# Gates of a linear recurrence: scaling inside the activations, a convolution tap on another engine, and work moved into the first head

## The chip, the cores and the metric

The kernel runs on one core of a Trainium2 chip. The metric is device time in microseconds, here from three runs of the unchanged kernel: median 2751.18 us, 2739.63 to 2753.92 us. The engines are TensorE (PE in the profile), VectorE (DVE), ScalarE (ACT), GpSimd (POOL) and the queue SyncE (SP).

## What is computed

One inference step of a decoder of two layers, for 512 prompt positions and 8 samples of one position each, 520 tokens in all. A layer projects the normed input with one large matrix, runs a retention branch (4 heads) and a gated linear recurrence (RG-LRU) on parts of the result, merges both, and ends with a SwiGLU block. The change is in the RG-LRU branch, of width 1280:

```
def causal_conv(x, buf, w, b):                   # CONV_W = 4
    xx = jnp.concatenate([buf, x], axis=1)
    y = b
    for j in range(CONV_W):
        y = y + xx[:, j:j + L] * w[j]
    return y, xx[:, -(CONV_W - 1):]

def rg_lru(xc, w_a, b_a, w_x, b_x, lam, h0):     # w_a, w_x block-diagonal, 16 blocks of 80
    r = sigmoid(xc @ w_a + b_a)
    i = sigmoid(xc @ w_x + b_x)
    log_a = -8.0 * r * softplus(-lam)
    a = jnp.exp(log_a)
    u = jnp.sqrt(-jnp.expm1(2.0 * log_a)) * (i * xc)
    # h_t = a_t * h_(t-1) + u_t, from h0
    return h, h[:, -1]
# lru_branch = (gelu(y_lru) * h) @ w_lru_out
```

## The kernel before

Everything lies transposed: 128 channels on the partitions, the 520 tokens along the free axis. Each float32 product is made of three TensorE passes (high x high, high x low, low x high; `product`, L321), so every operand is first split into a rounded high part and the rest. For weights GpSimd does the split, one unit of up to 1024 columns at a time: L307 makes `w_high`, L309 `w_low`, into two buffers that TensorE frees. SyncE loads the raw units. For activations ScalarE writes the high part (a Copy) and VectorE subtracts to get the low part.

Each engine runs an order that is written out by hand, and semaphores tie the engines together. TensorE's order in a layer is: four retention heads (the first in `one_head(0, True)`), two early tiles of the LRU's x branch, the eight output tiles of the last head (`ret_out`, added by VectorE in `ret_add`, L716), then the LRU stage, then merge, output projection and SwiGLU.

The LRU stage has 10 channel tiles, in two groups g of five (t = 0 to 4). For group 0 TensorE runs, for each t: `y` (8 blocks of 128x128, the gelu branch), two gate tiles (2 or 3 blocks each, from the convolved x), and one x tile (8 blocks) of a tile further on (`FILL_X`). Then come the x tiles (1,3) and (1,4), and group 1, where the place of the x tile is taken by output tiles `o` (5 blocks each, `FILL_O`). A block takes six matmuls of 260 columns. Results go through a ring of four PSUM places: the reader of place n must have freed it before TensorE may begin tile n+4. `read_x` (L877), `read_y` (L962) and `read_out` (L1009) on VectorE and the two sigmoids on ScalarE (L1300, L1303) are the readers.

For a tile c = 5g + t the work off TensorE is:

- `read_x`, then `conv`: the last tap with the bias (L894), three small copies for the outputs (L896 to L898), then per remaining tap one scalar_tensor_tensor over the prompt (L902) and one over the 8 sample columns (L904). ScalarE makes the high part (`conv_high`, L1291), VectorE the low part (`conv_low`, L911).
- ScalarE: two sigmoids. VectorE: `use_gates` multiplies r by the channel's 8 softplus (L969) and i by x (L972). ScalarE: a = exp(-.) (L1308), tanh (L1310), gelu of y (L1312). VectorE: `one_less_a2`, a squared (L979), then (a squared + 1) times tanh, which is 1 - a squared (L981). ScalarE: sqrt (L1314).
- VectorE: `scan` (L987 to L997) with a copy of the last columns (L995), then the split of the gated result (L1295, L1002).

Four of ScalarE's functions in this chain need a table load: sigmoid, exp (tanh shares it), gelu, sqrt. In VectorE's order `scan(g, t-1)` stands in the iteration of t. The softplus is a series (L919, L921, terms 19 down to 1 on 128x10), made by VectorE between the eight `ret_add`, from an exponential that ScalarE makes after the last head (L1280, L1282).

## Time and profile before

| what | value |
|---|---|
| median of 3 runs | 2751.18 us |
| the profiled execution: device time / span | 2757.06 us / 2755.3 us |
| TensorE matmuls busy | 2582.3 us, 94% |
| VectorE busy | 1467.1 us, 53% |
| ScalarE busy | 592.6 us, 22% |
| GpSimd busy | 1418.5 us, 51% |
| mean granted TensorE clock | 0.965 |

Times are read from one profiled execution. A busy share is an average over stages that have different limits; the LRU stage lies at about 560 to 840 us in layer 0 and 1930 to 2210 us in layer 1. The timelines give, for each instruction, its start, its length and in brackets how long its engine had been idle before it, and for whom it waited. "PEclk" is the granted TensorE clock as a share of full speed.

### The profile page before, as it was taken

What the parts mean: (1) busy time and instruction counts of PE and PEld (TensorE: products, weight loads), DVE (VectorE), ACT (ScalarE), POOL (GpSimd) and SP (SyncE); (2) the same over time, 40 slices, a digit from 0 to 9 for tenths busy, and PEclk for the clock granted to TensorE, in tenths of its full rate; (3) what the DMA queues carried; (4) which work ended last, traced back from release to release, by engine and by line L of the source; (5) the groups of instructions that cost most, each with busy time, mean ns of one, the idle gap of its engine ahead of it and who ended that gap; (6) DMA issues with size and microseconds to landing.
All of it is one profiled execution on the core that took longest, in us unless ns stands there. A gap on an engine that the chain in (4) does not pass through costs nothing.

```text
span 2755.3 us, 52731 instructions
## 1 busy us (share of the span) xinstructions
PE 2582.3 (94%) x20388; PEld 2539.4 (92%) x20388; DVE 1467.1 (53%) x1644; ACT 592.6 (22%) x825; POOL 1418.5 (51%) x845
## 2 busy tenths in 40 slices
PE   6999999988799999999999989899897999999997
PEld 6999999978799999999998989898797999999997
DVE  6554545388885553123346454545788845431333
ACT  2312121214451121001112030303144511210111
POOL 4262525245466666666642525262464666666664
PEclk9999999999899999999999989899998999999999
DMA  4534343522133322232335353435222333223322
GB/s 152 164 122 158 120 168 119 169 66 76 58 92 95 97 87 91 85 100 85 93 122 170 103 172 115 165 115 161 71 77 61 93 92 94 88 87 92 97 82 87
DMA packets 113048, 298.99 MB, mean 109 GB/s; under 512 B 11680, under 2 KB 12448, under 8 KB 112864
## 3 DMA queue, kind: packets, MB, share of 16 engines
q1 hardware_dynamic: 60480, 199.78, 23.4%
q10 hardware_dynamic: 52384, 96.56, 10.4%
q8 instruction: 140, 2.29, 0.3%
q14 instruction: 44, 0.36, 0.0%
HBM read 255.92 MB, written 40.38 MB: 108 GB/s over the span
## 4 chain that ended last, share of the span: by engine, by line
PE 68%; DVE 13%; DVEq 8%; issue 3%; DMA 3%; ACT 2%; ACTq 1%; POOL 1%; POOLq 1%
PE proj L321 42%; PE aux L321 19%; PE aux L527 3%; DVE scratch L902 2%; DVEq L1084 2%; DVEq L901 2%; DMA scratch<-in_sret 1%; PE aux L518 1%; DVE scratch L841 1%; PE aux L475 1%; POOL w_low L309 1%; PE aux L508 1%; DVE scratch L846 1%; ACTq L1355 1%; DVE scratch L704 1%
## 5 line engine op out<-in xcount | busy, mean ns | idle before, releaser
L307 POOL TENSOR_SCALAR w_high<-w_raw 128x1024 fp32r<-128x1024 f32 (+3 forms) x420 | 442.1, 1053 | 1251.3 <-PE proj L321 988.6
L309 POOL TENSOR_TENSOR w_low<-w_raw,w_high 128x1024 fp32r<-128x1024 f32 (+3 forms) x420 | 976.0, 2324 | 62.2 <-issue 3.5
L321 PE MATMUL proj<-x_high,w_high 128*128 128x260 f32 x3072 | 639.4, 290 | 71.4 <-DVE x_low L669 15.8
L321 PE MATMUL proj<-x_high,w_low 128*128 128x260 f32 x3072 | 627.7, 286 | 0.0
L321 PE MATMUL proj<-x_low,w_high 128*128 128x260 f32 x3072 | 627.6, 286 | 0.0
L321 PEld LDWEIGHTS proj<-x_high,w_high 128*128 128x128 f32 x3072 | 485.0, 193 | 80.5 <-issue 40.2
L321 PEld LDWEIGHTS proj<-x_low,w_high 128*128 128x128 f32 x3072 | 483.8, 193 | 0.0
L321 PEld LDWEIGHTS proj<-x_high,w_low 128*128 128x128 f32 x3072 | 483.1, 192 | 0.0
L321 PE MATMUL proj<-split_scratch,w_high 128*128 128x260 f32 x2368 | 386.7, 286 | 24.5 <-DVE scratch L877 11.4
L321 PEld LDWEIGHTS proj<-split_scratch,w_high 128*128 128x128 f32 x2368 | 328.1, 190 | 28.1 <-DVE scratch L877 11.9
L321 PE MATMUL aux<-split_scratch,w_high 128*128 128x260 f32 x1632 | 268.9, 288 | 23.9 <-DVE scratch L877 9.7
L321 PEld LDWEIGHTS aux<-split_scratch,w_high 128*128 128x128 f32 x1632 | 228.9, 193 | 25.8 <-issue 19.6
L321 PE MATMUL proj<-split_scratch,w_low 128*128 128x260 f32 x1184 | 240.4, 285 | 0.0
L321 PE MATMUL aux<-x_high,w_high 128*128 128x260 f32 x1024 | 206.8, 283 | 2.4 <-DVE residual L1076 1.6
L321 PE MATMUL aux<-x_high,w_low 128*128 128x260 f32 x1024 | 206.3, 283 | 0.0
L321 PE MATMUL aux<-x_low,w_high 128*128 128x260 f32 x1024 | 205.9, 283 | 0.0
L321 PEld LDWEIGHTS proj<-split_scratch,w_low 128*128 128x128 f32 x1184 | 184.6, 191 | 0.0
L321 PE MATMUL aux<-split_scratch,w_low 128*128 128x260 f32 x816 | 166.8, 286 | 0.0
L321 PEld LDWEIGHTS aux<-x_high,w_high 128*128 128x128 f32 x1024 | 157.9, 188 | 3.3 <-issue 2.0
L321 PEld LDWEIGHTS aux<-x_high,w_low 128*128 128x128 f32 x1024 | 157.8, 188 | 0.0
L321 PEld LDWEIGHTS aux<-x_low,w_high 128*128 128x128 f32 x1024 | 157.4, 188 | 0.0
L527 PEld LDWEIGHTS aux<-scratch 128*128 128x128 f32 x1024 | 131.1, 206 | 7.6 <-DVE scratch L813 6.5
(164 smaller groups left out, 2769.3 us busy)
## 6 DMA issues: line engine op xcount, KB each, us to landing
w_raw<-in_wstream SPq DMA_DIRECT2D x252, 512.0 KB, 3.5
scratch<-in_sret ACTq DMA_DIRECT2D x64, 512.0 KB, 6.4
out_ret_s<-scratch ACTq DMA_DIRECT2D x64, 512.0 KB, 6.1
w_raw<-in_wstream SPq DMA_DIRECT2D x72, 448.0 KB, 3.3
w_raw<-in_wstream SPq DMA_DIRECT2D x48, 384.0 KB, 3.0
scratch<-v_rows ACTq DMA_DIRECT2D x64, 256.0 KB, 5.0
w_raw<-in_wstream SPq DMA_DIRECT2D x48, 320.0 KB, 2.8
out_ret_p<-scratch ACTq DMA_DIRECT2D x8, 512.0 KB, 3.1
```

The source lines that it names most:

```text
L307: pool.tensor_scalar(WH[:, j, w], WR[:, j, w], 1.0, 0.0, ALU.mult, ALU.add)
L309: pool.tensor_tensor(WL[:, j, w], WR[:, j, w], WH[:, j, w].bitcast(F32), ALU.subtract).then_inc(s["w_split"], 1)
L321: m = pe.matmul(out, wt[:, w, blk * P:(blk + 1) * P], x[xi], start=first and n == 0, stop=last and n == 2)
L475: m = pe.matmul(AUX[:, BANK[N_SC + j], 0:SEQ - j * P], a[:, d, j * P:(j + 1) * P], b[:, d, j * P:SEQ], start=d == n == 0, stop=d == KT - 1 ...
L508: m = pe.matmul(AUX[:, BANK[N_AT + e], j * P:SEQ], a[:, j, e * P:(e + 1) * P], b[:, ST_OFF[j]:ST_OFF[j + 1]], start=j == n == 0, stop=j == ...
L518: m = pe.matmul(AUX[:, BANK[N_ST + d], :], a[:, j, d * P:(d + 1) * P], b[:, j, :], start=j == n == 0, stop=j == TT - 1 and n == 2)
L527: m = pe.matmul(AUX[:, BANK_SO, e * NS + b:e * NS + b + 1], SS[b % SRING][:, d, e * P:(e + 1) * P], QF[:, d, SEQ + b:SEQ + b + 1], start=b ...
L704: tt(SG[:, e, :], SG[:, e, :], RSTD, ALU.mult).then_inc(s["og_full"], 1)
L841: dve.tensor_reduce(SUM, OF.rearrange("p e t -> p t e"), AX.X, ALU.add).then_inc(s["gn_sum"], 1)
L901: dve.drain()
L902: stt(XCF[:, t, d:SEQ], xr[:, 0:SEQ - d], cw(j), XCF[:, t, d:SEQ], ALU.mult, ALU.add)
L1084: dve.drain()
```

## The change

- `r` is no longer multiplied by the softplus on VectorE: the factor is the per-channel scale of ScalarE's Exp and Tanh. The squared decay comes from an Exp of its own with twice the factor (`LAM` rows 4 and 5), so that `one_less_a2` is one instruction.
- The first convolution tap with its bias, the copies for the conv outputs and the copy of the scan's last columns are made on ScalarE (`first_tap`, `gated_high`); `XR` and `DF` get two buffers each.
- The three sample taps of all ten tiles are summed once per layer (`state_terms`, into `SCS`), in the first head; `conv` adds 8 columns. The series of the softplus is also made there, between the reads of the first head's v tiles (`series_begin`, `series_end`), and ScalarE's Abs and Exp for it stand in the first head.
- On VectorE `scan(g, t)` stands in the iteration of its own t, `read_x` ahead of it, and `gated_low(0, t)` at the iteration's end. On ScalarE `conv_high` stands between the sigmoids and the exponentials, one tile later than before. `conv(0, 0)` and `conv(0, 1)` follow `ret_add` 1 and 3 in place of 2 and 5.

TensorE's, GpSimd's and SyncE's orders are the same in both.

```diff
-        e_, z_, z2, acc = (DEC[:, LT * i:LT * (i + 1)] for i in range(4))
+        LAM = sb("lambda_series", [P, 6, LT])
+        e_, z_, z2, acc = (LAM[:, i, :] for i in range(4))
+        SCS = sb("conv_state_sum", [P, LT, NS])
+        SCT = sb("conv_state_term", [P, LT, NS])
...
-        DF, HF, XR = (FA[:, o + i * TOK:o + (i + 1) * TOK] for i in range(3))
-        assert o + 3 * TOK <= pos
+        DF, XR = (fview(o + 2 * i * TOK, 2, TOK) for i in range(2))
+        HF = FA[:, o + 4 * TOK:o + 5 * TOK]
...
+                    for n in (17, 15, 13):
+                        series(n)
+                def series_end():
+                    for n in (11, 9, 7, 5, 3, 1):
+                        series(n)
+                    tt(acc, acc, z_, ALU.mult)
+                    ts(e_, lam, -8.0, 0.0, ALU.mult, ALU.max)
+                    dve.drain()
+                    stt(lam, acc, 16.0, e_, ALU.mult, ALU.add)
+                    dve.drain()
+                    for n in range(2):
+                        ts(LAM[:, 4 + n, :], lam, -1.0 - n, None, ALU.mult)
...
+                def state_terms():
+                    dve.wait_ge(s["state_ld"], layer * 32 + 32)
+                    dve.wait_ge(s["small_st"], layer * 48 + 16)
+                    cw = CUR[:, PC_CW:PC_CW + LT * CW].rearrange("p (t j) -> p j t", j=CW)
+                    for j in range(CW - 1):
+                        term = SCT if j else SCS
+                        tt(term[:], SCV[:, :, j, :], cw[:, j].unsqueeze(2).broadcast_to([P, LT, NS]), ALU.mult)
+                        dve.drain()
+                        if j:
+                            tt(SCS[:], SCS[:], SCT[:], ALU.add)
+                            dve.drain()
+                    dve.tensor_copy(CVS[:, :, 0:CW - 2, :], SCV[:, :, 1:CW - 1, :])
...
+                        elif first:
+                            (series_begin, series_end, state_terms)[e - 1]()
...
                 def conv(g, t):
 
-                    early = g == 0 and t < X_EARLY
-                    xr = XR_EARLY[t] if early else XR
                     c = g * GT + t
-
-                    def cw(j):
-                        return CUR[:, PC_CW + c * CW + j:PC_CW + c * CW + j + 1]
-
-                    dve.drain()
-                    if not early:
-                        read_x(g, t, XR)
-                        dve.drain()
-                    ts(XCF[:, t, :], xr, cw(CW - 1), CUR[:, PC_CB + c:PC_CB + c + 1],
-                       ALU.mult, ALU.add)
-                    dve.tensor_copy(CVP[:, c, :], xr[:, SEQ - CW + 1:SEQ])
-                    dve.tensor_copy(CVS[:, c, 0:CW - 2, :], SCV[:, c, 1:CW - 1, :])
-                    dve.tensor_copy(CVS[:, c, CW - 2, :], xr[:, SEQ:TOK])
+                    xr = XR[:, c % 2, :]
+                    dve.wait_ge(s["tap_full"], layer * LT + (c + 1))
+                    tt(XCF[:, t, SEQ:TOK], XCF[:, t, SEQ:TOK], SCS[:, c, :], ALU.add)
                     for j in range(CW - 1):
                         d = CW - 1 - j
-                        dve.drain()
-                        stt(XCF[:, t, d:SEQ], xr[:, 0:SEQ - d], cw(j), XCF[:, t, d:SEQ],
-                            ALU.mult, ALU.add)
-                        m = stt(XCF[:, t, SEQ:TOK], SCV[:, c, j, :], cw(j), XCF[:, t, SEQ:TOK],
-                                ALU.mult, ALU.add)
+                        m = stt(XCF[:, t, d:SEQ], xr[:, 0:SEQ - d], CUR[:, PC_CW + c * CW + j:PC_CW + c * CW + j + 1],
+                                XCF[:, t, d:SEQ], ALU.mult, ALU.add)
+                        if j < CW - 2:
+                            dve.drain()
                     m.then_inc(s["xc_full"], 1)
...
                 for m_ in range(MT):
                     ret_add(tb0, C_X_EARLY + X_EARLY, m_)
-                    if m_ == 2:
+                    if m_ == 1:
                         conv(0, 0)
-                    elif m_ == 5:
+                    elif m_ == 3:
                         conv(0, 1)
-                        conv_low(0, 0)
-                    elif m_ == 0:
+                    elif m_ in (4, 5):
+                        conv_low(0, m_ - 4)
...
-                def use_gates(g, t):
-
-                    b, c, n = t % 2, g * GT + t, LRU_TILE["y", g, t]
-                    dve.wait_ge(*freed(layer, n + 1))
-                    ts(LA[:, b, :], LA[:, b, :], CUR[:, PC_SP + c:PC_SP + c + 1], None, ALU.mult
-                       ).then_inc(s["la_full"], 1)
+                def gate_input(g, t):
+                    b, n = t % 2, LRU_TILE["y", g, t]
                     dve.wait_ge(*freed(layer, n + 2))
                     tt(IX[:, b, :], IX[:, b, :], XCF[:, t, :], ALU.mult)
 
                 def one_less_a2(g, t):
 
-                    b = t % 2
-                    dve.drain()
-                    dve.wait_ge(s["th_full"], layer * LT + (g * GT + t + 1))
-                    tt(DF, AF[:, b, :], AF[:, b, :], ALU.mult)
-                    dve.drain()
-                    stt(DF, DF, 1.0, LA[:, b, :], ALU.add, ALU.mult).then_inc(s["d_full"], 1)
+                    b, c = t % 2, g * GT + t
+                    dve.wait_ge(s["th_full"], layer * LT + (c + 1))
+                    stt(DF[:, b, :], DF[:, b, :], 1.0, LA[:, b, :], ALU.add, ALU.mult).then_inc(s["d_full"], 1)
...
+                read_x(0, 2)
                 conv(0, 2)
-                conv_low(0, 1)
                 for t in range(GT):
                     read_y(0, t)
-                    if t:
-                        scan(0, t - 1)
-                        conv_low(*FILL_X[t - 1])
-                    else:
-                        conv_low(0, 2)
-                    use_gates(0, t)
-                    if t:
-                        gated_low(0, t - 1)
+                    conv_low(*((0, 2) if t == 0 else FILL_X[t - 1]))
+                    gate_input(0, t)
                     one_less_a2(0, t)
+                    read_x(*FILL_X[t])
+                    scan(0, t)
                     conv(*FILL_X[t])
-                scan(0, GT - 1)
+                    gated_low(0, t)
+                read_x(1, 3)
                 conv_low(*FILL_X[GT - 1])
                 conv(1, 3)
-                gated_low(0, GT - 1)
+                read_x(1, 4)
                 conv_low(1, 3)
                 conv(1, 4)
-                conv_low(1, 4)
...
+                    if first:
+                        A(e_, CUR[:, PC_SP:PC_SP + LT], ACT.Abs)
+                        act.drain()
+                        A(e_, e_, ACT.Exp, scale=-1.0).then_inc(s["lam_exp"], 1)
...
+                def first_tap(g, t):
+                    c = g * GT + t
+                    xr = XR[:, c % 2, :]
+                    act.wait_ge(s["xr_full"], layer * LT + (c + 1))
+                    A(CVP[:, c, :], xr[:, SEQ - CW + 1:SEQ], copy)
+                    A(CVS[:, c, CW - 2, :], xr[:, SEQ:TOK], copy)
+                    A(XCF[:, t, :], xr, ACT.Identity, bias=CUR[:, PC_CB + c:PC_CB + c + 1],
+                      scale=CUR[:, PC_CW + c * CW + CW - 1:PC_CW + c * CW + CW]).then_inc(s["tap_full"], 1)
...
+                    A(LRO[:, c, :], HF[:, SEQ - 1:TOK], copy)
...
-                    if t:
-                        gated_high(g, t - 1)
-                    act.wait_ge(s["la_full"], layer * LT + (c + 1))
-                    A(AF[:, b, :], LA[:, b, :], ACT.Exp, scale=-1.0)
+                def gate_decay(g, t):
+                    b, c, n = t % 2, g * GT + t, LRU_TILE["y", g, t]
                     act.drain()
-                    A(LA[:, b, :], LA[:, b, :], ACT.Tanh).then_inc(s["th_full"], 1)
+                    A(AF[:, b, :], LA[:, b, :], ACT.Exp, scale=LAM[:, 4, c:c + 1])
+                    A(DF[:, b, :], LA[:, b, :], ACT.Exp, scale=LAM[:, 5, c:c + 1])
+                    act.drain()
+                    A(LA[:, b, :], LA[:, b, :], ACT.Tanh, scale=CUR[:, PC_SP + c:PC_SP + c + 1]
+                      ).then_inc(s["th_full"], 1)
                     act.wait_ge(*freed(layer, n))
                     A(YF[:, b, :], YF[:, b, :], ACT.Gelu_apprx_tanh).then_inc(s["y_gelu"], 1)
                     act.wait_ge(s["d_full"], layer * LT + (c + 1))
-                    A(DF, DF, ACT.Sqrt).then_inc(s["w_sqrt"], 1)
-
-                for t in range(3):
+                    A(DF[:, b, :], DF[:, b, :], ACT.Sqrt).then_inc(s["w_sqrt"], 1)
+                act.wait_ge(s["og_low"], (layer + 1) * (HEADS * VT))
+                first_tap(0, 0)
+                first_tap(0, 1)
+                for t in range(2):
                     conv_high(0, t)
+                first_tap(0, 2)
                 for t in range(GT):
-                    gates(0, t)
-                    conv_high(*FILL_X[t])
+                    gate_sigmoids(0, t)
+                    conv_high(*((0, 2) if t == 0 else FILL_X[t - 1]))
+                    gate_decay(0, t)
+                    first_tap(*FILL_X[t])
+                    gated_high(0, t)
...
```

VectorE, group 0, an iteration of t = 1, from the product of i and x (before, L972) to the taps. Before:

```order
L972 TENSOR_TENSOR scratch<-scratch 128x520
L1002 TENSOR_TENSOR split_scratch<-scratch,split_scratch 128x520
L979 TENSOR_TENSOR scratch<-scratch 128x520
L981 SCALAR_TENSOR_TENSOR scratch<-scratch 128x520
L866 REGISTER_ALU
L877 TENSOR_TENSOR scratch<-proj,rinv 128x520
L894 TENSOR_SCALAR scratch<-scratch,params_cur 128x520
L896 COPY conv_p_sb<-scratch 128x3
L897 COPY conv_s_sb<-state_conv_sb 128x16
L898 COPY conv_s_sb<-scratch 128x8
L902 SCALAR_TENSOR_TENSOR scratch<-scratch,params_cur 128x509
L904 SCALAR_TENSOR_TENSOR scratch<-state_conv_sb,params_cur,scratch 128x8
```

After (L991 is `one_less_a2`, L932 `read_x`, L996 to L1005 `scan`, L940 and L943 `conv`):

```order
L991 SCALAR_TENSOR_TENSOR scratch<-scratch 128x520
L921 REGISTER_ALU
L932 TENSOR_TENSOR scratch<-proj,rinv 128x520
L996 TENSOR_TENSOR scratch<-scratch,state_lru_sb 128x8
L998 TENSOR_TENSOR scratch<-scratch 128x520
L1000 SCALAR_TENSOR_TENSOR scratch<-scratch 128x512
L1002 TENSOR_TENSOR scratch<-scratch 128x8
L1005 TENSOR_TENSOR scratch<-scratch 128x520
L939 REGISTER_ALU
L940 TENSOR_TENSOR scratch<-scratch,conv_state_sum 128x8
L943 SCALAR_TENSOR_TENSOR scratch<-scratch,params_cur 128x509
L943 SCALAR_TENSOR_TENSOR scratch<-scratch,params_cur 128x510
```

The product a times a, the first tap, the copies and the sample taps are gone, and the scan of the same tile now stands between the read of x and the taps.

ScalarE, the same iteration, from the second sigmoid to the high part of a convolved tile. Before (L1295 is `gated_high` of the tile before, L1291 `conv_high`):

```order
L1303 ACTIVATE scratch<-aux,params_cur 128x520
L1295 ACTIVATE split_scratch<-scratch 128x520
L1308 ACT_TABLE_LOAD
L1308 ACTIVATE scratch<-scratch 128x520
L1310 ACTIVATE scratch<-scratch 128x520
L1311 REGISTER_ALU
L1312 ACT_TABLE_LOAD
L1312 ACTIVATE scratch<-scratch 128x520
L1314 ACT_TABLE_LOAD
L1314 ACTIVATE scratch<-scratch 128x520
L1290 REGISTER_ALU
L1291 ACTIVATE split_scratch<-scratch 128x520
```

After (L1305 is `conv_high`, L1325, L1326 the two exponentials, L1328 tanh, L1331 gelu, L1333 sqrt):

```order
L1319 ACTIVATE scratch<-aux,params_cur 128x520
L1305 ACTIVATE split_scratch<-scratch 128x520
L1325 ACT_TABLE_LOAD
L1325 ACTIVATE scratch<-scratch,lambda_series 128x520
L1326 ACTIVATE scratch<-scratch,lambda_series 128x520
L1328 ACTIVATE scratch<-scratch,params_cur 128x520
L1330 REGISTER_ALU
L1331 ACT_TABLE_LOAD
L1331 ACTIVATE scratch<-scratch 128x520
L1333 ACT_TABLE_LOAD
L1333 ACTIVATE scratch<-scratch 128x520
L1295 REGISTER_ALU
```

`conv_high` moved from behind the sqrt to ahead of the exponentials, one Exp was added, and `first_tap` (from L1295 on) follows the sqrt. There are as many table loads as before.

VectorE, first head, the reads of the second to the fourth v tile and the first product with the decay. Before:

```order
L765 TENSOR_TENSOR scratch<-proj,rinv 128x520
L661 REGISTER_ALU
L765 TENSOR_TENSOR scratch<-proj,rinv 128x520
L661 REGISTER_ALU
L765 TENSOR_TENSOR scratch<-proj,rinv 128x520
L771 ISA
L776 TENSOR_TENSOR scratch<-aux,decay 128x512
```

After, from the read of the fourth v tile on (L765 to L770 is `state_terms`, L831 the product):

```order
L818 TENSOR_TENSOR scratch<-proj,rinv 128x520
L761 ISA
L765 TENSOR_TENSOR conv_state_sum<-state_conv_sb,params_cur 128x80
L765 TENSOR_TENSOR conv_state_term<-state_conv_sb,params_cur 128x80
L768 TENSOR_TENSOR conv_state_sum<-conv_state_sum,conv_state_term 128x80
L765 TENSOR_TENSOR conv_state_term<-state_conv_sb,params_cur 128x80
L768 TENSOR_TENSOR conv_state_sum<-conv_state_sum,conv_state_term 128x80
L770 COPY conv_s_sb<-state_conv_sb 128x10x16
L826 ISA
L831 TENSOR_TENSOR scratch<-aux,decay 128x512
```

Six instructions now stand between the last read of v and the first product with the scores; the series stands ahead of this, behind the second and the third read.

## Rows read from the trace of the kernel before

**Rows 1.** Windows by stage: length, busy us (instructions) per engine, PEclk, DMA share, GB/s.
```profile
560.00:840.00 280.00, 242.63 (x1891) 237.97 (x1889) 235.88 (x301) 113.17 (x135) 154.97 (x92) 0.95 0.25 76
...
840.00:1370.00 530.00, 527.79 (x4386) 526.89 (x4385) 200.59 (x197) 65.22 (x99) 329.48 (x207) 1.00 0.30 91
...
1930.00:2210.00 280.00, 243.58 (x1903) 239.44 (x1902) 233.51 (x300) 113.25 (x135) 157.85 (x94) 0.94 0.25 76
```

**Rows 2.** TensorE's waits in 560 to 840: us in total, times, longest.
```profile
PE proj L321 <- DVE scratch L877: 12.0, 3, 6.1
...
PE proj L321 <- DVE ret_acc L716: 6.8, 2, 3.9
...
PE aux L321 <- DVE scratch L877: 4.9, 1, 4.9
```

**Rows 3.** Timeline, TensorE, layer 0: start us, us, instruction, [idle before].
```profile
610.81 0.50 PE L321 MATMUL proj<-x_high,w_high 128*128 128x260 f32 x2 [2.86 <-DVE ret_acc L716]
...
627.06 1.21 PE L321 MATMUL aux<-split_scratch,w_high 128*128 128x260 f32 x4 [4.49 <-DVE split_scratch L911]
...
744.98 1.21 PE L321 MATMUL aux<-split_scratch,w_high 128*128 128x260 f32 x4 [4.87 <-DVE scratch L877]
...
752.70 0.75 PE L321 MATMUL aux<-split_scratch,w_high 128*128 128x260 f32 x4 [2.04 <-DVE scratch L962]
```

**Rows 4.** Windows of 10 us, same columns: after the two longest stalls.
```profile
740.00:750.00 10.00, 5.13 (x27) 5.05 (x27) 7.75 (x14) 1.16 (x2) 2.52 (x2) 0.55 0.05 9
```

**Rows 5.** Timeline, VectorE, LRU stage of layer 0.
```profile
622.98 0.75 DVE L902 SCALAR_TENSOR_TENSOR scratch<-scratch,params_cur 128x511 f32<-128x511 f32 x1
...
623.65 2.30 DVE L904 SCALAR_TENSOR_TENSOR scratch<-state_conv_sb,params_cur,scratch 128x8 f32<-128x8 f32 x1
...
644.03 0.22 DVE L904 SCALAR_TENSOR_TENSOR scratch<-state_conv_sb,params_cur,scratch 128x8 f32<-128x8 f32 x1
...
648.15 0.70 DVE L962 TENSOR_TENSOR scratch<-proj,rinv 128x520 f32<-128x520 f32 x1 [0.17 <-issue]
...
711.28 0.70 DVE L962 TENSOR_TENSOR scratch<-proj,rinv 128x520 f32<-128x520 f32 x1 [0.16 <-issue]
...
733.23 1.23 DVE L991 TENSOR_TENSOR_SCAN scratch<-scratch 128x512 f32<-128x512 f32 x1
```

**Rows 6.** Timeline, GpSimd, same stretch.
```profile
623.04 2.89 POOL L309 TENSOR_TENSOR w_low<-w_raw,w_high 128x1024 fp32r<-128x1024 f32 x1
...
640.05 2.10 POOL L309 TENSOR_TENSOR w_low<-w_raw,w_high 128x896 fp32r<-128x896 f32 x1
```

**Rows 7.** VectorE by line and shape: count | busy us, mean ns | idle before.
```profile
L904 DVE SCALAR_TENSOR_TENSOR scratch<-state_conv_sb,params_cur,scratch 128x8 f32<-128x8 f32 x60 | 45.6, 760 | 0.0
...
L969 DVE TENSOR_SCALAR scratch<-scratch,params_cur 128x520 f32<-128x520 f32 x20 | 21.7, 1086 | 5.3 <-ACT scratch L1300 5.3
...
L979 DVE TENSOR_TENSOR scratch<-scratch 128x520 f32<-128x520 f32 x20 | 23.6, 1181 | 7.3 <-ACT scratch L1310 5.8
...
L894 DVE TENSOR_SCALAR scratch<-scratch,params_cur 128x520 f32<-128x520 f32 x20 | 16.1, 808 | 1.9
...
L896 DVE COPY conv_p_sb<-scratch 128x3 f32<-128x3 f32 x20 | 15.4, 768 | 0.0
```

**Rows 8.** Timeline, ScalarE, LRU stage of layer 0.
```profile
636.02 1.28 ACT L1312 ACT_TABLE_LOAD   x1
...
637.31 0.64 ACT L1312 ACTIVATE scratch<-scratch 128x520 f32<-128x520 f32 x1
```

**Rows 9.** ScalarE by line and shape, columns as in 7.
```profile
L1342 ACT ACTIVATE scratch<-scratch,params_cur 128x520 f32<-128x520 f32 x32 | 23.2, 730 | 90.5 <-DVE scratch L1054 90.5
```

**Rows 10.** Timeline, VectorE, first head of layer 1.
```profile
1424.47 0.70 DVE L765 TENSOR_TENSOR scratch<-proj,rinv 128x520 f32<-128x520 f32 x1 [5.07 <-PE proj L321]
...
1431.65 0.69 DVE L776 TENSOR_TENSOR scratch<-aux,decay 128x512 f32<-128x512 f32 x1 [0.70 <-PE aux L475]
```

**Rows 11.** Timeline, VectorE: one step of the series, layer 0.
```profile
597.41 0.16 DVE L919 TENSOR_TENSOR decay<-decay 128x10 f32<-128x10 f32 x1
```

98 lines of the change are left out of this document (47 added, 51 removed).

## The prediction

> **What bounds the kernel now.** I read the windows by stage first. In the SwiGLU stage of layer 0 TensorE works 527.8 of 530 us, at a granted clock of 1.00; in the two LRU stages it works 242.6 and 243.6 of 280, at 0.95 and 0.94 [rows 1]. So there are some 37 us of idle TensorE per layer in this stage, and some time more at a lower clock. VectorE is busy for 235.9 of the same 280 us [rows 1]. Next, TensorE's waits there: all large ones name VectorE: `read_x` (12.0 + 4.9 us), `ret_add` (6.8) [rows 2], and one of 4.49 us for the low part of x [rows 3]. That is the sign of a stage in which VectorE sets the pace.
>
> Then the pace itself. `read_y` starts at 648.15 and, three iterations later, at 711.28 [rows 5]: 21.0 us an iteration. TensorE needs less: 527.79 us for 4386 matmuls is 0.1203 us each, 0.722 for a block of six; an iteration of 22 blocks is 15.9 us. From 610.81 (first ring tile) to 752.70 (second output tile) [rows 3] it has 147 blocks, 106.1 us, and takes 141.9. After this point hardly a wait is left, so this time and the eight `ret_add` before it are what the change can win.
>
> Why does VectorE take so long? Its instruction on 8 columns (L904) takes 0.22 us at 644.03 but 2.30 at 623.65; it then ends at 625.95, and GpSimd's L309, begun at 623.04, ends at 625.93 [rows 5, 6]. So a VectorE instruction that reads SBUF waits for GpSimd's to end. The mean of L904 is 0.76 us, not 0.22 [rows 7]. Adding up the lengths of the instructions of an iteration that met no such wait (0.22, 0.70, 0.75, the scan's 1.23 [rows 5]; estimates of 0.5 for a tensor_scalar and 0.16 for a copy) I get 12.4 us, 13.4 with drains. So 7.6 us of 21.0 are waits for GpSimd: 0.6 us per us of work.
>
> **What each edit is worth.**
>
> *Removed from VectorE, per tile.* By the means: the first tap 0.81, the copy of 3 columns 0.77, three sample taps 2.28, the product with the softplus 1.09, a squared 1.18 [rows 7]: 6.1 us, against some 0.5 for the one new 8-column addition (0.22 to 0.76). By the unhindered lengths it is 2.6 us. These are the two bounds, since a wait for GpSimd that one instruction is spared may simply fall on the next. The first gives 21.0 - 6.1 + 0.5 = 15.4 us, under TensorE's 15.9; the second 18.4, and to that any new wait for ScalarE is added.
>
> *Moved: the chain of an iteration.* The scan is now in its own tile's iteration and `conv_high` ahead of the exponentials, so there is a loop through both engines: taps done, `conv_high`, three activations with a factor, gelu, sqrt, then on VectorE product, scan, product, then the next tile's taps. On ScalarE: 0.64, load 1.28, three at 0.73 (the length of an activation with an operand from the parameters [rows 9]), load 1.28, 0.64, load 1.28, 0.64 [rows 8] = 7.95 us. VectorE's part: 0.70 + 1.23 + 0.2 + 0.70 and drains, 3.0, and taps 0.22 + 3 x 0.75 and drains, 2.7 [rows 5]. 5.7 us at 0.6 of waiting per us add 3.4. Together 17.1. In ScalarE's 7.95 us VectorE has five other instructions of 0.70 and one of 0.17 to do, 3.7 us, with drains and waiting some 6.5: just hidden. I take 17.3 us an iteration.
>
> *Added to ScalarE.* One Exp, the tap (0.73) and three small copies, some 2 us a tile. It is busy for 113.2 of 280 us [rows 1], 20 more is nothing as a load; the Exp counts because it is in the loop, and is in the sum. The tap begins once sqrt is done, while VectorE scans: hidden. If VectorE were to get there first, it would cost up to 1.2 us a tile.
>
> *The `ret_add` part.* The series and two full convs no longer stand between the additions. The new conv (2.7 us, with waiting 4.3) and an addition fit nearly into two tiles of TensorE (5.8 us). I count the 6.8 us of waits as gone, and 2 us of low clock behind them: 9 us a layer. The first ring tile starts at 601.8.
>
> *From there to the second output tile.* Gates of tile 0 done after 20 blocks, 616.3. Then sigmoid, the ScalarE chain: sqrt done at 624.9. Scan and taps with waiting, 8.9: 633.8. Four iterations of 17.3: 703.0. Then two convs and their reads (each: read 0.7, tap on ScalarE 1.2, taps, low part, some 7), then `read_y`: 717.5. Before: 752.70 [rows 3]. Gained 35.2, with the 9 in it. TensorE still waits three or four times for some 3 us; before, after waits of 6 and 4.87 us the granted clock was 0.55 [rows 4], close to the 1.2 GHz level. For the shorter waits I take 1.5 us off: 33.7 a layer. In group 1 I count nothing: TensorE has no waits to speak of there, and VectorE gets lighter.
>
> *The first head.* VectorE is idle for 5.07 us between the reads of v [rows 10]. A step of the series is two instructions of 0.16 [rows 11] with drains, 0.49 us: the first part some 3 us, the second 6 x 0.49 + 1 = 3.9, with waiting 6 or so: the fourth v tile is read 1 us late at the worst. `state_terms`, six instructions of up to 160 columns, stands ahead of the first product with the scores, which begins at 1431.65 [rows 10] and frees the bank that the transposes wait for. It costs between 0 (if TensorE's scores take as long) and 4 us. I take 1.5 us a layer.
>
> *Sum.* 2 x 33.7 - 2 x 1.5 = 64.4 us. Against the profiled execution, 2757.06 us (span 2755.3), that is 2692.7. The median of the runs, 2751.18, lies 5.9 under it; I forecast 2690, between the two bases.
>
> **A rule that speaks against it.** The row: a table load is 1.28 us from 636.02, and the gelu begins at 637.31 [rows 8]. So a switch costs 1.29 us here, and the loop above has three of them. The Trainium skill, "ScalarE: Activation LUTs", What ACT_TABLE_LOAD costs, adds a drain of about 1.38 us to each load of about 1.28. By that the loop would be 4.1 us longer. The row shows no such drain, so the trace disagrees.
>
> **Rivals.**
>
> *The port sets the pace (28%).* GpSimd's two instructions of a unit take 2.89 or 2.10 us for the second and about 1 for the first [rows 6]: three units make some 9.5 us an iteration. VectorE's remaining instructions that read SBUF are 8.0 us. If they exclude each other all the time, 17.5 us is the floor, and with the waits for ScalarE 20. For it: VectorE's waiting did not come from its own small instructions. Against: VectorE now waits for ScalarE at times, and GpSimd works then. Price: 4 x 2.7 = 10.8 us a layer more, 2714.
>
> *TensorE sets the pace (18%).* The means are the truth, the iteration falls to 15.9. Then 35.8 + 9 - 3 for the convs ahead of group 1 = 42 us a layer, less the first head: 2676. Against: the loop of 17.
>
> *The loads cost twice (3%).* If ScalarE's gaps open as VectorE's waits come closer, by 1.28 for each of three loads, the iteration is 21.1 and only 9 and some 7 us a layer are gained: 2726. This is the place where the skill's drain would show.
>
> *Slower (4%).* The early scan exposes ScalarE: VectorE, in strict order, stands at the wait for sqrt with `read_x`, the taps and the next `read_y` queued behind it, and TensorE's ring with them. If nothing is hidden in those 7.95 us, an iteration is 10.7 us of work, 7.5 of waiting for GpSimd and 7.95: 26.2. Five times 8.9 is 44.5 us, more than the 35.2: 9.3 us a layer lost, with low clock and the first head some 12: 2780. It decides from an iteration of 24.4 us on.
>
> *The change does less than it says (2%)*: the three small copies on ScalarE delay the taps so that each tile waits 1.2 us for them; 12 us a layer, 2716.
>
> **Numbers.** The forecast has 45%. The range 2662 to 2722 takes in TensorE's pace and the port's. Its lower end is near the case with no stall at all (35.8 + 9 - 0 = 44.8 a layer, 2667, from the lower base 2662). Under 0.5% (14 us) counts as no change: faster 0.92, same 0.04, slower 0.04.
>
> **What would show it.** Right: `read_y` in group 0 at 17 to 18 us intervals; TensorE's waits in the stage down from 37 to 10 to 15 us, named `read_x`, `read_y`; VectorE waiting some 1 us for sqrt in each iteration; no wait for `ret_add`; the second output tile at about 717. The port: intervals of 20 with VectorE still busy for 90% in them. TensorE's pace: intervals of 15.9. In the first head a wait of TensorE of 1 to 2 us ahead of the transposes. Wrong: a wait for sqrt of over 5 us, or one in group 1.

## The result and the profile after

The changed kernel takes 2683.82 us (median of 4 runs, 2671.31 to 2686.85), the kernel before 2749.99 (4 runs, 2739.63 to 2753.92). The ratio is 0.9758, interval [0.9733, 0.9784]. The forecast was 2690. The profiled execution took 2686.85 us with a span of 2685.0.

Windows by stage, columns as in [rows 1]: the LRU stage of layer 0, the SwiGLU stage, the LRU stage of layer 1.

```profile
560.00:840.00 280.00, 267.26 (x2161) 264.25 (x2160) 201.70 (x198) 134.34 (x188) 179.85 (x106) 0.98 0.28 86
840.00:1370.00 530.00, 519.61 (x4293) 518.17 (x4293) 201.69 (x199) 64.59 (x97) 323.31 (x202) 0.99 0.31 95
1890.00:2170.00 280.00, 268.29 (x2162) 264.94 (x2163) 202.22 (x200) 134.86 (x189) 180.25 (x106) 0.98 0.29 86
```

TensorE was idle for 37.4 us of the 280 and is now idle for 12.7; its clock there rose from 0.95 to 0.98. VectorE's instructions fell from 301 to 198, its busy time only from 235.9 to 201.7.

TensorE's waits in the same stretch (compare [rows 2]); L978 is `read_y`, L720 `ret_add`:

```profile
PE proj L325 <- DVE scratch L978: 6.0, 3, 3.8
PE aux L325 <- DVE scratch L978: 1.9, 1, 1.9
PE proj L325 <- DVE ret_acc L720: 1.0, 2, 0.8
```

The waits for `read_x` (16.9 us) are gone, since `read_x` now stands ahead of the scan. What is left is for `read_y`, and 1.0 us for `ret_add`. It is still VectorE that is late, at one place an iteration.

The timeline of TensorE, at four places: the start of the retention tiles, two waits for `read_y`, and the second output tile (752.70 in [rows 3]).

```profile
573.12 0.90 PE L325 MATMUL proj<-split_scratch,w_high 128*128 128x260 f32 x4 [1.74 <-DVE split_scratch L714]
...
670.41 0.50 PE L325 MATMUL proj<-x_high,w_high 128*128 128x260 f32 x2 [1.79 <-DVE scratch L978]
...
688.79 0.50 PE L325 MATMUL proj<-x_high,w_high 128*128 128x260 f32 x2 [3.78 <-DVE scratch L978]
...
716.51 0.94 PE L325 MATMUL aux<-split_scratch,w_high 128*128 128x260 f32 x4 [1.93 <-DVE scratch L978]
```

One iteration on VectorE, from `read_y` of tile 2 to that of tile 3 (answers to [rows 5]):

```profile
651.67 0.70 DVE L978 TENSOR_TENSOR scratch<-proj,rinv 128x520 f32<-128x520 f32 x1 [0.16 <-issue]
...
654.93 2.47 DVE L991 SCALAR_TENSOR_TENSOR scratch<-scratch 128x520 f32<-128x520 f32 x1 [1.16 <-ACT scratch L1328]
...
658.84 0.97 DVE L998 TENSOR_TENSOR scratch<-scratch 128x520 f32<-128x520 f32 x1 [0.53 <-ACT scratch L1333]
659.88 3.27 DVE L1000 TENSOR_TENSOR_SCAN scratch<-scratch 128x512 f32<-128x512 f32 x1
...
664.51 1.81 DVE L940 TENSOR_TENSOR scratch<-scratch,conv_state_sum 128x8 f32<-128x8 f32 x1
666.24 2.39 DVE L943 SCALAR_TENSOR_TENSOR scratch<-scratch,params_cur 128x509 f32<-128x509 f32 x3
...
669.58 0.70 DVE L978 TENSOR_TENSOR scratch<-proj,rinv 128x520 f32<-128x520 f32 x1 [0.17 <-issue]
```

VectorE waits for tanh (L1328) and for sqrt (L1333). The scan, 1.23 us alone, takes 3.27 here; the one addition on 8 columns takes 1.81. And the ScalarE chain beside it (answers to [rows 8]), from the high part of the convolved tile (L1305, for which it waits for VectorE's taps) to the sqrt:

```profile
650.75 0.64 ACT L1305 ACTIVATE split_scratch<-scratch 128x520 fp32r<-128x520 f32 x1 [3.65 <-DVE scratch L943]
...
654.17 0.73 ACT L1328 ACTIVATE scratch<-scratch,params_cur 128x520 f32<-128x520 f32 x1
654.92 1.28 ACT L1331 ACT_TABLE_LOAD   x1
656.21 0.64 ACT L1331 ACTIVATE scratch<-scratch 128x520 f32<-128x520 f32 x1
656.87 1.28 ACT L1333 ACT_TABLE_LOAD   x1
658.16 0.64 ACT L1333 ACTIVATE scratch<-scratch 128x520 f32<-128x520 f32 x1
```

Two of its loads, with gaps of 0.02 us at most around them. The chain takes 8.05 us, and VectorE's product (L998, 658.84) begins 0.04 us after the sqrt has ended: the loop of the forecast is there to be seen.

VectorE's groups in 560 to 840 (busy us, mean ns; answer to [rows 7]):

```profile
L943 DVE SCALAR_TENSOR_TENSOR scratch<-scratch,params_cur 128x509 f32<-128x509 f32 (+2 forms) x30 | 33.3, 1109 | 1.5
L1000 DVE TENSOR_TENSOR_SCAN scratch<-scratch 128x512 f32<-128x512 f32 x10 | 17.5, 1753 | 0.7
L991 DVE SCALAR_TENSOR_TENSOR scratch<-scratch 128x520 f32<-128x520 f32 x10 | 15.1, 1510 | 8.2 <-ACT scratch L1328 8.2
L940 DVE TENSOR_TENSOR scratch<-scratch,conv_state_sum 128x8 f32<-128x8 f32 x10 | 13.7, 1366 | 1.4 <-ACT scratch L1298 1.4
```

The 8-column addition has a mean of 1.37 us, where each of the three instructions that it replaces had 0.76 [rows 7]. A part of the waiting for GpSimd has moved onto what is left; how much, the runs with GpSimd on 8 columns show below.

### The profile page after: what moved, and what is told of

It is laid out like the page before. It is cut to its first block, busy times and chain, and to the rows that moved or that the text cites. A ratio compares the mean times of both kernels' runs of the same rounds, so it can differ in the third digit from the quotient of the medians.

```text
span 2685.0 us, 52601 instructions
## 1 busy us (share of the span) xinstructions
PE 2561.6 (95%) x20388; PEld 2521.4 (94%) x20388; DVE 1396.5 (52%) x1480; ACT 629.4 (23%) x925; POOL 1422.3 (53%) x845
## 3 DMA queue, kind: packets, MB, share of 16 engines
q10 hardware_dynamic: 52384, 96.56, 10.6%
## 4 chain that ended last, share of the span: by engine, by line
PE 69%; DVE 12%; DVEq 6%; issue 3%; ACT 3%; DMA 3%; ACTq 2%; POOL 1%; POOLq 1%
PE proj L325 42%; PE aux L325 20%; PE aux L531 3%; DVE scratch L943 2%; DVEq L1087 2%; DMA scratch<-in_sret 2%; DVEq L946 1%; PE aux L522 1%; DVE scratch L896 1%; PE aux L512 1%; POOL w_low L313 1%; DMA out_ret_s<-scratch 1%; PE aux L479 1%; DVE scratch L901 1%; ACTq L1387 1%
```

## A measure that leaves the heads out

The six intervals between the group norms of successive heads, which the change does not touch, add up to 857.1 us in the profile of before and 845.5 in that of after. A single one takes between 136 and 145 us in the profiles of this study; in the twelve further ones the six sum to 835 to 850, as in after's, and before's sum is the longest of the fourteen. The length goes with the granted clock: before's six intervals have 0.94 to 0.96, the three under 138 us in the two runs of the better version below have 0.99. The two kernels that were profiled twice gave the same sum within 1.5 us, so whether the difference is chance is open. So 11.6 us of the 70.3 us between the two profiled executions are not shown to be the change's. I therefore read from each profile:

- the *stretch*: in layer 0, from the first matmul of the eight last retention tiles to the first of the second output tile: before 578.00 to 752.70, 174.7 us; after 573.12 to 716.51, 143.4. It holds 1074 matmuls in every kernel (in layer 1 it is 175.7 and 143.5);
- the time *outside the heads*: from the last group-norm sum of a layer to the first product with the decay of the next, or to the end: before (1431.65 - 559.18) + (2755.3 - 1924.57) = 1703.2 us; after (1398.01 - 554.28) + (2685.0 - 1885.84) = 1642.9.

The medians are of 4 to 10 runs, or one run where the text says so; the stretch and the time outside the heads are each read from one profile.

| kernel | median us | stretch | outside the heads |
|---|---|---|---|
| before | 2749.99 | 174.7 | 1703.2 |
| scaling and square in the activations alone | 2736.31 | 171.6 | 1696.8 |
| softplus and sample taps in the first head alone | 2722.60 | 162.7 | 1678.1 |
| the same, and the new order | 2705.13 | 156.0 | 1667.2 |
| all parts, old order | 2704.19 | 153.8 | 1662.6 |
| after, scaling and square back on VectorE | 2697.30 | 146.0 | 1650.2 |
| after (again) | 2683.82 (2682.52) | 143.4 (143.6) | 1642.9 (1640.7) |
| after, `read_y` early | 2680.88 | 142.3 | 1639.4 |
| after, `read_y` and gelu early (again) | 2669.47 (2670.21) | 138.8 (139.1) | 1628.7 (1629.1) |
| after, longer ScalarE chain | 2692.38 | 148.8 | 1651.2 |
| before, GpSimd on 8 columns | 2619.41 | 129.6 | 1596.6 |
| after, GpSimd on 8 columns | 2620.12 | 129.0 | 1596.6 |

## The experiments

### The parts alone

*The softplus series and the sample taps in the first head, all else as before* (the functions of the kernel after, called between the reads of v):

```diff
+                        elif first:
+                            (series_begin, series_end, state_terms)[e - 1]()
```

> The kernel before with one part of the change alone: the series of the softplus and the sample taps are made in the first head. The stretch from the first matmul of the eight last retention tiles to the first matmul of the second output tile was 174.7 us before and 143.4 after. Theory (VectorE and GpSimd shut each other out, and VectorE's own work sets the pace): three 8-column instructions become one, 0.4 us an iteration unhindered, 1.8 by their means, and the eight additions are no longer held up by the series: stretch 163 to 169, whole kernel 12 to 22 us faster, first head at most 0.5 us a layer longer. Rival (the order is what gained): stretch 172 or more, whole kernel within 8 us of before.

Measured 2722.60 us (2707.27 to 2726.33), ratio 0.9905 [0.9867, 0.9943]; stretch 162.7, outside the heads 25.1 us less. Theory, and a little more than it gave (25.9 us below the median of the kernel before beside it, for 12 to 22). This is the largest part. Of the 12.0 us of the stretch 6.4 are gained before the first ring tile, among the additions that the series had held up (26.4 us for 32.8), and 0.5 us in each interval. Of the two waits for `ret_add` in [rows 2] the one of 3.9 us is gone, the other takes 2.7. The `read_y` intervals are 20.6 (638.65 to 700.39), and the waits for `read_x` stay, as this row of its TensorE timeline shows:

```profile
725.75 1.24 PE L324 MATMUL proj<-split_scratch,w_high 128*128 128x260 f32 x4 [4.05 <-DVE scratch L928]
```

*The scaling and the square inside the activations, all else as before:*

```diff
-                    A(AF[:, b, :], LA[:, b, :], ACT.Exp, scale=-1.0)
...
+                    A(AF[:, b, :], LA[:, b, :], ACT.Exp, scale=LAM[:, 0, c:c + 1])
+                    A(DF[:, b, :], LA[:, b, :], ACT.Exp, scale=LAM[:, 1, c:c + 1])
```

> The kernel before with one part of the change alone: the softplus factor as the scale of Exp and Tanh, and a squared by an Exp of its own. Theory (VectorE's work sets the pace): two instructions fewer, 1.2 us an iteration unhindered, 2.3 by their means (1.09 + 1.18), so intervals of read_y of 18.7 to 19.8 in place of 21.0, stretch 164 to 170, whole kernel 10 to 20 us faster. Rival (the order is what gained): stretch 172 or more, kernel within 8 us.

Measured 2736.31 us (10 runs, 2729.37 to 2748.09), ratio 0.9964 [0.9944, 0.9984]. By the ratio that is 9.9 us (4 to 15), at the lower edge of the expected span. The last three `read_y` intervals average 19.9 us (649.43 to 709.06) for 21.0: two full VectorE operations, 2.3 us by their means, gave 1.2 us an iteration, which is their length unhindered and close to the expectation's bound. The stretch is 171.6 all the same, and neither theory has that: the first `read_y` comes 2.3 us later behind the first addition (581.64 to 629.15 for 581.81 to 626.98), with the two small instructions in between that make the scaled factors; that these are the cause isn't shown. Outside the heads it is 6.4 us, 0.3 for each of the 20 tiles, since in group 1 a shorter VectorE gains nothing (from its first `read_y` to its last 57.1 us before and 57.6 here); the heads' sum was 847.9 against 857.1.

*The same part undone in the kernel after:*

```diff
+                    ts(LA[:, b, :], LA[:, b, :], CUR[:, PC_SP + c:PC_SP + c + 1], None, ALU.mult
+                       ).then_inc(s["la_full"], 1)
...
+                    tt(DF[:, b, :], AF[:, b, :], AF[:, b, :], ALU.mult)
+                    dve.drain()
```

> The kernel after, with one part undone: the scaling of r and the square of a are VectorE operations again (two of 128x520 more an iteration, one exponential of ScalarE less). In the old order this part was worth 13.7 us (2749.99 - 2736.31). Theory A (the part is worth the same in any order, its VectorE work at the port-hindered price less what ScalarE gives back): 2695 to 2701, stretch 146 to 150. Theory B (in the new order both operations lie on the loop that sets the interval, between sigmoid and exponential and between tanh and square root, with nothing beside them): 2 x 0.70 hindered to 1.1 or 1.2 each plus a hand-over, less 0.73 of ScalarE, so intervals of 19.3 to 20.3, stretch 151 to 156, 2703 to 2715.

Measured 2697.30 us (2694.21 to 2707.41), ratio 0.9835 [0.9794, 0.9877]; stretch 146.0, intervals 18.6 (637.97 to 693.69). Theory A: the part is worth much the same in either order, 6.4 us outside the heads in the old and 8.4 in the new (1650.2 - 1641.8, the mean of after's two profiles). VectorE then hardly waits for ScalarE at all: the wait ahead of 1 - a squared, 3.8 us in 600 to 700 after, becomes this:

```profile
DVE scratch L994 <- ACT scratch L1332: 1.0, 2, 0.8
```

So work and wait change places, and only the difference counts.

### The order

*All parts, with the old order of both engines* (scan of the tile before, `conv_high` behind sqrt, the first two convs behind additions 2 and 5):

```diff
                     read_y(0, t)
-                    conv_low(*((0, 2) if t == 0 else FILL_X[t - 1]))
+                    if t:
+                        scan(0, t - 1)
+                        conv_low(*FILL_X[t - 1])
+                    else:
+                        conv_low(0, 2)
                     gate_input(0, t)
+                    if t:
+                        gated_low(0, t - 1)
                     one_less_a2(0, t)
                     read_x(*FILL_X[t])
-                    scan(0, t)
                     conv(*FILL_X[t])
-                    gated_low(0, t)
```

> The changed kernel with the instruction order of before on VectorE and ScalarE (scan one iteration late, conv_high behind sqrt, convs at additions 2 and 5), all other parts of the change kept. Theory A (a loop through both engines sets the pace): in this order the loop is gated_high, exponentials, sqrt, first tap, conv, read_y, scan: 19.2 us by the lengths of the rows; stretch 148 to 153, kernel 8 to 18 us slower than the changed one. Theory B (the port shared with GpSimd alone sets it): the same instructions stand in the port, so the intervals stay at 17.8 and the stretch at 142 to 146; within 5 us of the changed kernel. Theory C (the order is the main gain): stretch above 160.

Measured 2704.19 us (2701.36 to 2709.15), ratio 0.9856 [0.9836, 0.9875]: 20.4 us slower than after, more than either theory gave. Stretch 153.8, intervals 19.3 (628.86 to 686.88), where theory A had 148 to 153 and 19.2. VectorE waits for the first tap (600 to 700 us), and TensorE's waits for `read_x` are back (560 to 840):

```profile
DVE scratch L940 <- ACT scratch L1306: 11.3, 5, 3.1
```

```profile
PE proj L325 <- DVE scratch L932: 6.0, 2, 4.4
PE aux L325 <- DVE scratch L932: 4.2, 1, 4.2
```

*The order without the work moved to ScalarE* (the kernel after, with scaling, square, first tap and copies back on VectorE):

```diff
-                    dve.wait_ge(s["tap_full"], layer * LT + (c + 1))
+                    ts(XCF[:, t, :], xr, CUR[:, PC_CW + c * CW + CW - 1:PC_CW + c * CW + CW],
+                       CUR[:, PC_CB + c:PC_CB + c + 1], ALU.mult, ALU.add)
```

> The order of the kernel after with only the softplus and the sample taps in the first head: scaling, square, first tap and the small copies are VectorE's again. It differs from the first-part run (stretch 162.7 us, 2722.6) by the order alone, and from the run with scaling and square back (146.0, 2697.3) by the first tap and copies alone. In the profiles, the time outside the heads (from layer 0's last group-norm sum to layer 1's first head, and from layer 1's last one to the end) was 1703.2 before, 1678.1 with the first part, 1662.6 with all parts in the old order, 1642.9 after. Theory A (the order is worth its 20 us by itself: TensorE's tiles are read out before the long VectorE work, whatever that work holds): 1655 to 1661 outside the heads, stretch 150 to 154, 2698 to 2707. Theory B (the order pays only once the first tap is ScalarE's, since the VectorE tap stands between the early read and the taps and fills the time that the order set free): 1667 or more outside the heads, stretch 157 or more, 2710 or more.

Measured 2705.13 us (2703.41 to 2710.93), ratio 0.9852 [0.9830, 0.9873]; stretch 156.0, outside the heads 1667.2. The time is theory A's, the time outside the heads theory B's, the stretch between them: the order alone is worth 10.9 us outside the heads (1678.1 - 1667.2), with the tap on ScalarE about 20 (1662.6 - 1641.8). Equally the first tap with its copies is worth 17.0 in the new order (1667.2 - 1650.2), and about 9 in the old, if the other two parts add up there (1703.2 - 25.1 - 6.4 - 1662.6). Each is worth nearly twice as much with the other: in the old order VectorE stands and waits for the tap (the 11.3 us above), in the new one it scans meanwhile. In the order in which they were added, the parts are 25.1 + 10.9 + 17.0 + 8.4 = 61.4 us.

### What sets the interval: the loop, or GpSimd

*A longer chain*: the second exponential made three times, on ScalarE alone.

```diff
-                    A(DF[:, b, :], LA[:, b, :], ACT.Exp, scale=LAM[:, 5, c:c + 1])
+                    for k in range(3):
+                        A(DF[:, b, :], LA[:, b, :], ACT.Exp, scale=LAM[:, 5, c:c + 1])
+                        if k < 2:
+                            act.drain()
```

> The changed kernel with the second Exp made three times, which adds 2 x 0.71 us and two drains to ScalarE's part of the loop in each of the ten tiles. Theory A (the loop sets the pace): intervals of 19.2 to 19.4 in place of 17.8, stretch 7 to 8 us longer, 151. Theory B (the port sets it, ScalarE is hidden): intervals within 0.4 of 17.8, stretch 143 to 145.

One execution: 2692.38 us, stretch 148.8 in both layers, `read_y` intervals 18.9 (641.62 to 698.19). Between the theories, and nearer to A. `read_y` isn't in the loop itself, though. From the first high part (L1305 after) to the one behind tile 4's taps the five iterations take 19.2 us each (620.43 to 716.39), where they take 17.6 in the first profile of after (614.51 to 702.72) and 18.1 in the second (617.16 to 707.88). The chain is 1.6 us longer (9.65 for 8.05), so between 1.1 and 1.6 of it arrive: the loop sets the pace. VectorE's waits for tanh and sqrt grew (600 to 700 us):

```profile
DVE scratch L991 <- ACT scratch L1331: 10.1, 4, 2.8
DVE scratch L998 <- ACT scratch L1336: 6.8, 4, 2.1
```

(3.8 and 2.6 us after.)

*GpSimd's two instructions of a weight unit on 8 columns*, in the kernel before and in the kernel after. The split of the weights is left out; they are the constant 0.01.

```diff
-                j, w = (base + k) % 2, slice(0, n * P)
+                j, w = (base + k) % 2, slice(0, 8)
```

> The kernel before, but GpSimd's two instructions of each unit work on 8 columns; the weights' high and low parts are a constant 0.01 throughout, so the product's values are other ones. It leaves out the split of the weights. Theory (VectorE instructions that read SBUF wait for GpSimd's, 7.6 of 21.0 us an iteration): VectorE's iteration falls to 13.4 us, under TensorE's 15.9, the small instructions take 0.22 and not 0.76 us on average, and the stretch of 174.7 us falls to TensorE's own 131 to 137. Rival (VectorE's long means come from its own drains and from ScalarE): 165 or more.

> The changed kernel, GpSimd on 8 columns as in the run before it, the weights' parts a constant 0.01. Theory: without GpSimd the two kernels are alike in this stage, both at TensorE's pace: stretch 131 to 136 (143.4 with GpSimd), at most 3 us from the run before it; what the change gained was VectorE's time under GpSimd's load. Rival (the loop through ScalarE binds even so): 138 or more, and more than the unchanged kernel without GpSimd.

2619.41 and 2620.12 us, one execution each (the kernel before beside them 2751.64): without GpSimd's work the change is worth nothing. Both have the same time outside the heads, and TensorE waits 0.3 us and not at all in the stretch, which is 1 to 2 us shorter than the theories gave. Windows 560 to 840 of the two, before and then after:

```profile
560.00:840.00 280.00, 279.65 (x2331) 279.42 (x2331) 159.61 (x326) 118.75 (x144) 32.87 (x116) 1.00 0.31 92
```

```profile
560.00:840.00 280.00, 280.00 (x2337) 280.00 (x2336) 129.76 (x206) 133.65 (x189) 31.64 (x114) 1.00 0.31 93
```

`read_y` comes every 15.86 and 15.85 us, TensorE's own pace (forecast 15.9). These windows hold more work than those with GpSimd's full load. For what VectorE waits, the same instructions have to be compared, from the first `ret_add` of the last head to the last `read_y` of layer 0 (some 260 instructions before, some 152 after). First the kernel before, whole and with GpSimd on 8 columns:

```profile
581.81:809.00 227.19, 194.44 (x1502) 190.91 (x1501) 189.89 (x260) 93.69 (x109) 121.78 (x75) 0.93 0.24 71
...
567.71:748.42 180.71, 180.36 (x1502) 180.13 (x1501) 117.19 (x259) 93.61 (x109) 22.29 (x74) 1.00 0.30 90
```

then the kernel after, the same two:

```profile
577.82:774.69 196.87, 186.49 (x1505) 184.09 (x1504) 152.26 (x152) 109.30 (x151) 123.56 (x75) 0.98 0.27 83
...
564.92:744.96 180.04, 180.04 (x1502) 180.04 (x1501) 93.33 (x153) 109.29 (x151) 22.73 (x74) 1.00 0.30 90
```

VectorE's busy time is 189.9 us against 117.2, and 152.3 against 93.3: the waiting for GpSimd is 72.7 us before and 58.9 after, 0.62 and 0.63 us for each us of VectorE's own work. The waiting shrinks with the work: 23.9 us of own work less took 13.8 us of waiting with it. In the three iterations from `read_y` of tile 1 to that of tile 4 it is 8.0 us an iteration before and 6.7 after. The loop and GpSimd are thus not alternatives: the same ScalarE chain as in the kernel after stands in the run with GpSimd on 8 columns, but without the waiting VectorE's part of the loop (product to last tap) takes 5.2 us and not 9.5, short enough for the loop to close within 15.85 us. (That constant weights alone raise the clock was not tested apart.)

### A better version

*`read_y` of the next tile ahead of the taps; and with it the gelu ahead of the sigmoids*, where ScalarE waits for TensorE, and out of the chain between tanh and sqrt:

```diff
                     scan(0, t)
+                    if t < GT - 1:
+                        read_y(0, t + 1)
                     conv(*FILL_X[t])
```

```diff
                 def gate_sigmoids(g, t):
                     b, c, n = t % 2, g * GT + t, LRU_TILE["y", g, t]
+                    act.wait_ge(*freed(layer, n))
+                    A(YF[:, b, :], YF[:, b, :], ACT.Gelu_apprx_tanh).then_inc(s["y_gelu"], 1)
                     r_done(n + 1)
...
-                    act.wait_ge(*freed(layer, n))
-                    A(YF[:, b, :], YF[:, b, :], ACT.Gelu_apprx_tanh).then_inc(s["y_gelu"], 1)
```

Both edits, then the first alone, then both and the kernel after once more on one chip:

> The changed kernel with read_y of the next tile ahead of the convolution, and gelu ahead of the sigmoids, so that the loop is 1.9 us shorter on ScalarE (one table load of 1.28 and 0.64), with the same work for every engine. Theory A (the loop sets the pace of 17.8 us): intervals of 16.0 to 16.8, TensorE's waits for read_y gone, stretch 135 to 139, kernel 8 to 16 us faster than the changed one. Theory B (the port sets it): intervals 17.3 or more, only the waits for read_y go: stretch 140 to 143, 0 to 5 us faster.

> The kernel after, with read_y of the next tile ahead of the convolution's taps on VectorE, and the gelu where it was (behind the tanh). It splits the gain of the run with both edits (2669.47 us, stretch from the first matmul of the eight last retention tiles to the first of the second output tile 137.4 us, against 2683.82 and 143.4). Theory A (the slot that read_y frees is what TensorE waits for, 3.9 us of taps stood ahead of it): nearly all of the gain is here, stretch 138 to 140, 9 to 13 us under the kernel after. Theory B (the loop through ScalarE sets the interval, and a read further ahead only moves the wait): stretch 141 to 143, intervals of read_y within 0.3 of 17.8, 1 to 5 us under the kernel after.

> The kernel with read_y ahead of the taps and the gelu ahead of the sigmoids once more, beside the kernel after on the same chip. If its gain over the kernel after is real: 2666 to 2673, 10 to 17 us under the kernel after measured next to it, stretch 136 to 139. If it was chance of the heads' clock: within 5 us of it.

> The kernel after, unchanged, as the partner of the run before it: 2679 to 2688, stretch 142 to 145 and read_y intervals of 17.6 to 18.0 in the first layer. Where 11.6 us of the first comparison came from the six intervals between heads that the change doesn't touch, this shows whether they come out at 139 or at 144 us again: if by chance, the split among the twelve differs from before, and the LRU part stays within 1 us of where it was.

Both: 2669.47 us, ratio 0.9735 [0.9711, 0.9759]; again 2670.21 (6 runs, 2660.17 to 2676.70), ratio 0.9726 [0.9693, 0.9759]. The kernel after beside it: 2682.52 (6 runs, 2673.36 to 2696.79), 0.9777 [0.9740, 0.9814]. So 12 to 14 us are gained, 12 to 14 of them outside the heads; the two latter intervals overlap slightly, the pairs of medians and the profiles agree twice. Time and stretch are as theory A had them, the intervals are not: the last three are 17.6 us (625.57 to 678.28) for 16.0 to 16.8. In three of the five iterations VectorE's product no longer starts with the end of the sqrt but later, behind VectorE's own work, so that of the 1.9 us taken out of the chain not all can come back. `read_y` early alone gives 2680.88 (2674.28 to 2685.13), ratio 0.9762 [0.9722, 0.9803]: theory B by time and stretch, 142.3. The last three intervals are 18.5 us (627.14 to 682.55), all four 17.7 (after's four, the first of 23.0 with them, 19.1). TensorE's waits for `read_y` almost vanish, and one for `read_x` takes their place:

```profile
683.38 0.50 PE L325 MATMUL proj<-x_high,w_high 128*128 128x260 f32 x2 [0.75 <-DVE scratch L978]
...
706.73 1.24 PE L325 MATMUL proj<-split_scratch,w_high 128*128 128x260 f32 x4 [4.34 <-DVE scratch L932]
```

With the gelu early too, VectorE's wait for sqrt in 600 to 700 falls from 5.0 us to 0.7, and TensorE's for `read_x` (second run) to:

```profile
700.75 0.75 PE L325 MATMUL proj<-split_scratch,w_high 128*128 128x260 f32 x4 [2.76 <-DVE scratch L932]
```

My expectation for the second run of after held in time, stretch and intervals; in layer 1 the stretch was 141.6 for 143.5, more than the 1 us allowed. The six intervals between heads again sum to 845.5, in another split (139.2, 140.5, 140.6, 142.5, 139.7, 143.0 for 139.0, 139.6, 142.6, 143.2, 140.7, 140.4). For both edits the sums are 835.1 and 836.6. Whether that is chance is open.

## Why the prediction was right, step by step

*What bounds the stage.* Right: VectorE, and through GpSimd. The runs with GpSimd on 8 columns show it outright, and put the waiting at 0.62 and 0.63 us per us of work over the whole stage, where 0.6 was read from one iteration. TensorE's idle time in the stage fell from 37.4 to 12.7 us (forecast 10 to 15).

*The interval.* Forecast 17.3, measured 17.76 (634.68 to 687.96, three of them) and 17.95 in the second profile; the one ahead of these, 611.67 to 634.68, is 23.0 us (21.2 before), outside the 17 to 18 that were to show the forecast right. The loop itself, from the end of tile 0's taps (631.99) to that of tile 4's (702.63), takes 17.66. The chain of ScalarE was right to the row, 8.05 for 7.95, and "just hidden" held: in all five iterations the product starts 0.03 to 0.04 us after the sqrt's end. The term that was too small is VectorE's part of the loop, product to last tap: 9.4, 10.6, 9.8, 10.2 and 7.5 us, 9.5 in the mean for 9.1, since its 5.2 us of own work (with GpSimd on 8 columns) draw some 0.8 us of waiting per us and not 0.6. VectorE's wait was put at the wrong place: in the iteration shown two thirds of it is for tanh (1.16 us), and only 0.53 for sqrt.

*The retention part.* Forecast 9 us; measured 6.6: from the first retention matmul to the first ring tile 32.8 us before (578.00 to 610.81), 26.2 after (573.12 to 599.30). The two convs took 5.3 and 5.1 us (581.32 to 586.57 and 587.70 to 592.76) for 4.3 forecast, and left waits of 0.80 and 0.16; and TensorE ran the first 10 us at a granted clock of 0.83, where it had 1.00 before, though the same wait of 1.74 us for the group norm stands ahead of them in both. In the second profile of after, with clock 1.00 there, this part takes 25.2 us; the rest of the stretch is 1.1 us longer in it, and the whole is 143.6 all the same. Whether one brings the other about isn't shown.

*To the second output tile.* Forecast 717.5, measured 716.51; but layer 0's heads ended 4.9 us earlier, so of the forecast 35.2 us the stretch gave 31.3. The 3.9 us fall on the retention part (2.4), the first scan and taps (0.7) and four iterations of 17.66 for 17.3 (1.4), less 0.6 at the end. Per layer the time outside the heads fell by 30.2 us (31.3 by the second profile of after), where 33.7 was forecast.

*The first head.* Forecast 1.5 us a layer, with a wait of 1 to 2 us ahead of the transposes. The wait is in both layers, at half the size or less. From the first matmul of the scores to the first behind the transposes TensorE takes 5.5 us before (73.80 to 79.29) and 6.4 after (74.00 to 80.40), in both layers and both profiles of after: it cost 0.9 us a layer. (The end of the first head can't be used for this: in the two profiles of after it comes at 133.0 and 138.5 us, before at 132.6.)

```profile
PE aux L487 <- DVE scratch L831: 0.7, 1, 0.7
```

*The sum.* Outside the heads 60.3 us against 67.4 forecast (2 x 33.7), 1.6 lost in the first heads up to their last group-norm sum against 3.0, and 11.6 from the heads' intervals, which no term foresaw: 60.3 - 1.6 + 11.6 = 70.3. So the mechanism was right and the gain outside the heads some 10% too large. That the medians lie 66.2 us apart (2749.99 - 2683.82), so near to the 64.4 of the sum, is in part luck: the heads of before were the slowest of all profiles and made up for what the terms had too much. The median came out 6.2 us under the forecast.

*The rivals.* The port as the pace (intervals of 20) and TensorE's pace (15.9) did not come, though the second is what both kernels do without GpSimd. The slower case did not: the wait for sqrt is 0.5 us, not 7.95, though in strict order VectorE does stand at it. The case in which the loads cost twice did not, see below; nor the one of the small copies: VectorE waits 1.4 us in all for the first tap (L940, ten tiles), where it was to be 1.2 in each. In group 1 there is a wait for sqrt (3.3 us in five, 0.8 at the longest), which was to count against the forecast; TensorE doesn't wait there for it, so the sign was chosen badly.

*The drain.* The Trainium skill, "ScalarE: Activation LUTs", What ACT_TABLE_LOAD costs, has a load of about 1.28 us and a drain of about 1.38. The loads are 1.28 in the rows above, with no gap over 0.02 ahead of them or behind; the trace agrees with the first and shows nothing of the second. By the page's figures the interval would have been 21.4 (an estimate: 17.3 and three drains).

## What to carry to other kernels

Where one engine's instructions wait for another's, the mean length of an instruction is not what it gives back when removed: two full VectorE operations per tile, 2.3 us by their means, gave 1.2 us an iteration, and nothing in the tiles where TensorE did not wait for VectorE anyway, so that the whole kernel got 0.3 us a tile. Compare the same instructions, not the same window, when you price such waiting. Find the loop through the engines (here chain, scan, taps, next high part), count it, and look for work in it that could stand where an engine waits anyway: the gelu moved out of the chain was worth more (10 to 11 us) than the scaling and the square moved into the activations (6 to 8). And try early what the kernel takes with the suspected neighbour's work nearly gone; here this showed that 130 us of 2750 hang on GpSimd, and that the change shortens work that waits for GpSimd and leaves the cause in place.
